# Context normalisation in fewer picks, and its key and value blocks 5.33 picks apart, in a two-layer diffusion backbone

## The reference

```python
for i in range(2):
    hx = hx + gate * mixer_i(modulate(hx, norm1_g[i], shift, scale))
    hx = hx + gate * peer(modulate(hx, norm2_g[i], ...))      # 8 heads x 16 experts of 16384
    if i == 0:
        hc = hc + gate * pool(modulate(hc, ...)); hc = hc + gate * peer(modulate(hc, ...))
# mixer_1 projects both hx and modulate(hc, norm1_g[1], ...) to q, k, v, z, a, b:
#   k, v = silu(conv5(h @ w_in)); decay g = -exp(a_log) * softplus(a + dt_bias); beta = sigmoid(b)
# from the context only k, v, g and beta are needed: its last states start the latents' scan
return rmsnorm(hx, final_g)
```

## Time and profile before

| what | value |
|---|---|
| median of three runs | 2551.62 us |
| the profiled execution's own time | 2557.68 us |
| its span | 2555.7 us |
| TensorE busy (matmul) | 2161.7 us, 85% |
| VectorE busy | 1900.9 us, 74% |
| ScalarE busy | 1103.8 us, 43% |
| GpSimd busy | 921.4 us, 36% |
| mean DMA rate | 361 GB/s |
| granted TensorE clock, mean | 0.976 |

### The profile page before, as it was taken

The page is one execution under the profiler, slowest core; times in us unless marked ns, Lnnn a source line. Parts: engine busy times, 40 slices in busy tenths (PEclk is TensorE's granted clock), DMA queues, the critical chain, the costliest instruction groups (busy, mean ns, idle before and its releaser), DMA issues.

```text
span 2555.7 us, 33277 instructions
## 1 busy us (share of the span) xinstructions
PE 2161.7 (85%) x11048; PEld 1182.1 (46%) x11048; DVE 1900.9 (74%) x5194; ACT 1103.8 (43%) x3063; POOL 921.4 (36%) x902
## 2 busy tenths in 40 slices
PE   7789987787887789888899898998879977777777
PEld 4545542343443344444445457977755522232222
DVE  6667887877877787887887878955577766777674
ACT  5445543433434345554435443633344434344333
POOL 0033333333333435554343434621223333333332
PEclk9899999999999999999999999999989999999999
DMA  9499999999999999999999996800269999999997
GB/s 365 148 403 420 411 421 420 415 408 409 418 408 420 406 405 418 418 418 400 385 381 405 377 400 234 301 19 2 94 266 420 414 422 421 417 417 417 416 411 307
DMA packets 142536, 923.53 MB, mean 361 GB/s; under 512 B 16449, under 2 KB 16609, under 8 KB 43169
## 3 DMA queue, kind: packets, MB, share of 16 engines
q0 software_dynamic: 111696, 810.17, 77.4%
q1 hardware_dynamic: 30672, 111.31, 11.5%
HBM read 920.35 MB, written 1.06 MB: 361 GB/s over the span
## 4 chain that ended last, share of the span: by engine, by line
PE 22%; DMA 20%; DVE 12%; issue 5%; ACT 3%; POOL 2%; POOLq 0%; DVEq 0%
DMA buf<-in_experts,buf 20%; PE pY L2539 12%; DVE buf L1622 5%; PE pY L2299 3%; PE pG L2299 2%; POOL lo L2127 2%; PE pS L2299 1%; PE pS L2271 1%; PE pS L2272 1%; PE pS L2273 1%; ACT buf L813 1%; ACT buf L834 1%; DVE buf L1443 1%; PE pY L2271 1%; PE pY L2272 0%
## 5 line engine op out<-in xcount | busy, mean ns | idle before, releaser
L2539 PE MATMUL pY<-buf 128*128 128x512 f32 x3072 | 1473.5, 614 | 319.3 <-ACT buf L834 316.1
L2108 POOL DMA_INDIRECT buf<-in_experts,buf x768 | 752.0, 979 | 1286.4 <-PE pY L2539 1227.6
L2539 PEld LDWEIGHTS pY<-buf 128*128 128x128 f32 x3072 | 543.2, 191 | 1148.0 <-ACT buf L834 704.1
L1622 DVE SCALAR_TENSOR_TENSOR buf<-pS,buf 128x1024 f32<-128x1024 f32 x384 | 468.5, 1222 | 228.8 <-DMA buf<-in_experts,buf 225.6
L1622 DVE SCALAR_TENSOR_TENSOR buf<-pG,buf 128x1024 f32<-128x1024 f32 x384 | 469.0, 1223 | 223.6 <-DMA buf<-in_experts,buf 218.5
L828 ACT ACTIVATE buf<-buf 128x1 f32<-128x1 f32 x768 | 154.8, 202 | 1034.6 <-DVE buf L1622 1033.3
L813 ACT ACTIVATE buf<-ident,buf 128x128 f32<-128x128 f32 x768 | 296.8, 386 | 0.0
L834 ACT ACTIVATE buf<-buf 128x128 f32<-128x128 f32 x768 | 296.7, 386 | 0.1
L2271 PE MATMUL pY<-h_hi,hi 128*128 128x256 f32 x480 | 151.7, 316 | 8.8 <-DVE h_lo L1278 7.0
L2272 PE MATMUL pY<-h_lo,hi 128*128 128x256 f32 x480 | 137.2, 286 | 0.0
L2273 PE MATMUL pY<-h_hi,lo 128*128 128x256 f32 x480 | 137.1, 286 | 0.0
(11 more groups left out here) (382 smaller groups left out, 2476.4 us busy)
## 6 DMA issues: line engine op xcount, KB each, us to landing
raw<-in_blocks SPq DMA_DIRECT2D x104, 512.0 KB, 7.4
buf<-in_mod_tiles SPq DMA_DIRECT2D x30, 512.0 KB, 5.3
g<-in_mod_tiles SPq DMA_DIRECT2D x26, 512.0 KB, 8.1
buf<-in_experts,buf POOLq DMA_INDIRECT x768, 10.5
raw<-in_mod_wT SPq DMA_DIRECT2D x20, 512.0 KB, 7.3
buf<-in_mod_wT SPq DMA_DIRECT2D x20, 512.0 KB, 8.2
buf<-in_window SPq DMA_DIRECT2D x2, 1024.0 KB, 11.2
buf<-in_keysT POOLq DMA_DIRECT2D x2, 1024.0 KB, 5.1
```

The lines of the kernel that those rows point to most:

```text
L1622: v.scalar_tensor_tensor(x, h_tok[NT * i // NPICK], 1.0, x, ALU.mult, ALU.mult, accum_out=dots[:, i:i + 1]).then_inc(dotted, 1)
L2108: g_.indirect_dma_start(rows_uv[n % ROW_RING].rearrange("p a d -> p (a d)"), None, table, bass.IndirectOffsetOnAxis(expert[:, i:i + 1].bit ...
L2539: mm = t_.matmul(pY[:, 2 * r + hf, :], diags[:, i % DIAG_RING], rows_uv[n % ROW_RING][:, 1, GRP * hf:GRP * hf + GRP], start=(k == 0), stop ...
```

## The change

The context's residual, norm and split take fewer picks of x's call, the first key and value block stands at pick 33 instead of 38, and block `j` stands `16 * j // 3` picks after it instead of `5 * j`: 33, 38, 43, 49, 54, 59, 65, ... 113 for 38, 43, 48, ... 113. The last one stays at 113.

```diff
-NORM_PICK = (96, 22)
+NORM_PICK = (96, 18)
-KV_STEP = 5
+KV_FIRST = 33
 def kv_pick(j):
-    return 38 + KV_STEP * j
+    return KV_FIRST + 16 * j // 3
 # ScalarE
-                    if g == 1 and i == TOPK + 1:
+                    if g == 1 and i == TOPK - 1:
                         norm(4, res[1], lambda: act.wait_ge(fin_ready, 2))
-                    if after and i == (112, 32)[g]:
+                    if after and i == (112, 28)[g]:
                         act.wait_ge(h_tokens, NT * (g + 1))
                         act.wait_ge(normed, 4 + g)
                         h_high(after, 0)
 # VectorE
-                    if g == 1 and i in (12, 15):
-                        q = (i - 12) // 3
+                    if g == 1 and i in (12, 14):
+                        q = (i - 12) // 2
                         ve.wait_ge(y_chan, q + 1)
                         add_branch(res[1], y_half, 0, 5, 1, fin_ready, 4 * q, 4 * q + 4)
-                    if g == 1 and 25 <= i < 31:
-                        norm_ctx(i - 25)
+                    if g == 1 and i in (21, 24, 25, 26):
+                        for part in ((0,), (1,), (2, 3), (4, 5))[(21, 24, 25, 26).index(i)]:
+                            norm_ctx(part)
-                    if after and 0 <= i - (120, 34)[g] < 4:
-                        h_low_part(g + 1, after, i - (120, 34)[g])
+                    if after and 0 <= i - (120, 29)[g] < 4:
+                        h_low_part(g + 1, after, i - (120, 29)[g])
 # TensorE
-                    if i == 35 + r:
+                    if i == 28 + r:
                         pe.wait_ge(normed, 5)
-                    if g == 1 and i in (10, 13):
-                        ctx_transposed((i - 10) // 3)
+                    if g == 1 and i in (10, 12):
+                        ctx_transposed((i - 10) // 2)
```

## The result

The changed kernel is slower by 0.35%: its time is 1.0035 times that before, 95% interval [1.0020, 1.0049]. The medians of six runs each are 2563.61 us (2559.67 to 2570.78) and 2553.02 us (2551.35 to 2562.69); the ratio puts it at +9 us. Forecast were +1.8 us and 2553.4, with a range up to 2560: the time lies outside it, on the side of the second rival.

What follows compares the result with a forecast made beforehand. DMA transfers were taken as the bound. Terms +1.2 + 0.8 + 0.3 - 0.5 = +1.8 us on the median 2551.6 gave 2553.4 us; forecast -1.5 to +4.5 (2550.1 to 2556.1) at 0.62, range 2547 to 2560.

Steps and rivals of the forecast that it cites:

- the second rival: TensorE's wait for `gl_x` before block 1 drains the DMA queue: +5 to +8.5 us, 2556.6 to 2560.1, chance 0.18.
- The bound: From 865 to 1155 us transfers at 423 GB/s are the bound; an ideal schedule could win 6.1 us.
- Norm, +1.2: Picks 15 to 22: mean one pick behind h's transposing, picks 5.7 us late against 4.5; bounds 0 and +3.4.
- First block at 33, second at 38: TensorE waits 3.9 us for `gl_x` behind pick 38, delaying row 45's gather: +0.8 us, bounds 0 and 3.1.
- Then 2.9 us of block: Block 1 on TensorE, right behind the wait at pick 38, was taken to last 2.9 us.
- Row 45's late issue: Gather behind block 1 and pick 39 goes out at 969.3 instead of 966.21, landing at 976.5 to 977.6; costs 0.7 to 1.8.
- Its signs: TensorE stands over 3 us behind pick 38 and row 45 lands more than 9 us after pick 39's end.
- the norm at +3.4: Upper bound for the mean behind h's transposing, picks 17 to 22, if none of that transposing is covered: +3.4 us.
- Blocks 5.33 apart, -0.5: Picks 33 to 113: wider spacing fits TensorE and frees some of 2.8 us; -0.5 us, bounds -2.8 and 0.
- Never on the long step: VectorE's taps fall at picks 4, 5, 9, 10, 14, 15 of a head, avoiding the long step at 7.
- ScalarE at 53 to 57, +0.3: Silu moved from 59 to 55 among six table loads: 15.3 us of work in 13.7 of transfers; bounds 0 and +1.6.
- The signs named beforehand: 865 to 1155 no shorter, deep slices 8 us earlier, TensorE idle behind pick 38, row 45 late, 418 to 423 GB/s from pick 60.

Runs made afterwards that it cites:

- the decay at 34: Changed kernel with VectorE's whole decay step at pick 34 instead of 39, so block 1's bank is free earlier; 1.0015 of before, 2560.91 us.
- the early bank: Changed kernel with only the decay's first product, which reads the a/b bank, moved to step 32 with its own signal; 1.0028 of before, 2564.57 us.
- the decay at 45: Kernel before with the decay at step 45 instead of 39, so block 1 at 43 waits for its bank; 1.0019 of before, 2561.73 us.
- h at 23: The early bank's kernel with h's transposing moved from pick 17 to 23, behind the mean; 1.0017 of before.
- the decay at 44: Kernel before with the decay at step 44 instead of 39, behind block 1 at 43; 1.0000 of before, 2555.62 us.

## Why the prediction was wrong

**The bound: right.** Transfers are; 423 GB/s holds wherever no hole is, and every loss found is a hole of them.

**Norm, +1.2: right.** Picks 18 and 20 and the mean ended as reckoned (910.6, 918.7, 914.1, by the timeline). The stretch lost 2.2 us more, and alone it measures +1.8 us, not clear of zero. That the nearness of two long pieces is the cause can't be shown by time: pulled apart, it stays at 1.0007.

**First block at 33, second at 38, +0.8 with bounds 0 and 3.1: this step failed.** Its wait is there as forecast, 3.67 us for 3.9, released by VectorE. Its price is not: 4.9 us (2.3 to 7.7) put alone into the kernel before, 6.6 us taken out by the decay at 34, 3.3 us (not clear of noise) by the early bank. The holes behind the wait miss 3.6, 5.8 and 4.4 us of transfer in three traces, all above the bound of 3.1. What was mis-sized:

- *The block was priced at full clock.* "Then 2.9 us of block" came from a row in which TensorE had no idle time before it. Behind the wait it took 4.5 us at a granted clock of 0.51 to 0.64 (in the kernel before with the decay at 45, at 0.50, it took 5.5 us from first start to last end, where a block at full clock takes 3.4). The Trainium skill (TensorE: Matmul & The Clock Gate, "What's actually happening") gives an idle TensorE the lower clock. The trace agrees, with 0.51 behind 3.67 us without work. The bounds should have held such a block.
- *Row 45's late issue was taken as 3.1 us.* Pick 39 ended at 973.6, not 968.9, and row 45 went out at 973.96, 7.8 us late. Of this 2.3 us were there at row 44 already; they are about what the norm's hole had cost every row, and are no new loss. (The prediction had named the norm's cost and left VectorE's step at its old time: "the decay, whose last operation ends at 964.16" ended at 967.15, behind a dot of pick 39 that started at 961.33 for 958.68.) The other 5.5 us are the wait's: the 3.1 forecast, 1.6 for the clock, and the rest for VectorE, which ran a little later still and whose cast at L1452 took 0.88 us for 0.33, mostly beside GpSimd's issue of row 44.
- *The price was read off one landing.* The forecast priced the late issue by when row 45 lands. By that measure it was right: with the queue empty the row landed 5.6 us after its issue, sooner than the 7.2 us reckoned with, and so 1.5 us behind where the shift of 2.3 us and one more block put it (978.1), inside the forecast's 0.7 to 1.8. But an empty queue shortens the landing of the first row only. The transfers that should have run in 972 to 976 are missing all the same, 3.6 us of them, and row 46 is 5.9 us later than before where row 45 is 5.0.

The second rival, "the wait for `gl_x` drains the queue", +5 to +8.5 us at 0.18, names what happened: slices of 33 and 4 GB/s. Its signs were badly chosen. TensorE standing over 3 us was already met by the forecast's own 3.9 us. Row 45 landing more than 9 us after pick 39's end did not come: it was 6.0 us (979.55 behind 973.6), since a drained queue makes a landing short and not long. The argument against it, that six row buffers keep bytes in the queue, fails since all six wait for the same TensorE. Its other part, the norm at +3.4, did not come, and its "whole 3.1 us" was too little for the wait.

**Blocks 5.33 apart, -0.5: no gain shows.** With wait and norm accounted for, 1.0015 - 1.0007 = 0.0008 is left of the kernel with the decay at 34, 2 us, within both uncertainties; with the early bank it is 0.0021, 5.4 us. Whether the spacing costs or the move of the blocks to earlier picks can't be told apart: spacing 5 from pick 33 was no better, with a loss of its own behind pick 108. Where the blocks fall within a head seems to matter (a pick later, the rate rises from 403 to 413 GB/s), but the times don't settle it. "Never on the long step" was counted for one engine, while the blocks' parts on ScalarE and GpSimd moved onto others: in the changed kernel VectorE's search met the low parts, and block 10 (pick 86) stood right behind a gate exponential at 85.

**ScalarE at 53 to 57, +0.3: not contradicted.** In the changed kernel itself no dip stands there: from 1005 to 1035 its two traces miss 0.2 and 0.3 us, the kernel before 0.6. With the early bank a hole of 3.1 us stands at 1015 to 1023; with the decay at 34 under 1 us is missing there, with the norm alone nothing. The silu is not the whole cause, as the hole stays when it is moved; what is, stays open.

**The signs named beforehand.** Right: 865 to 1155 no shorter, the deep slices some 10 us earlier, TensorE's idle time and its releaser, row 45 late, no dip near pick 55. Wrong: the slices are deeper than before (57 GB/s where the lowest was 180), and "from pick 60 on 418 to 423 GB/s" fails in the first trace by the hole at 1104. Behind pick 113 the rows catch up by 2.2 us from row 120 to row 152; the kernel with the norm alone, its blocks in their old places, catches up by 3.3, so the blocks are not the reason.

**What stays open.** By the medians the 10.5 us split into 1.8 for the norm, 3 to 7 for the wait and 2 to 5 for the place of the blocks; each part is known no better than to 2 or 3 us. The two ways of removing the wait differ by 3.3 us, within their intervals, and both leave a hole near 972. That a late start from the norm is part of this hole is shown by one trace only (h at 23). The sums of a/b in another bank weren't tried. And 9 us by the ratio stand against 2 us between the two profiles, of which the rows 12 to 120 explain 6.7: single executions differ by several us between the calls too, where this change does nothing.

## What to carry to other kernels

Before a piece of work is moved ahead of a wait that used to be long over, lay out all five engines at the new place: when the signal comes there, what the waiting engine's next piece takes if its clock has fallen, and whether all buffers hang on that engine. Add up everything that is late in the same few microseconds, from the last issue that went out in time, before subtracting the queue's slack. Price a late issue by the transfers that are missing and not by when the late one lands. In these traces the stand-still cost no transfer while it lasted, and showed as a hole in the DMA rate some 5 to 10 us later, so look for the cause ahead of the hole.

And where two executions differ elsewhere by more than the change is worth, compare them over the stretch that it touches, from a gather ahead of it to a gather behind it.

## What the runs showed of the hardware

TensorE's granted clock fell to half behind 3.67 us without work (0.51 from 969 to 971) and behind 4.64 us (0.50 from 980 to 984), in the middle of a busy stretch; the block of 24 matmuls behind it took 1.6 and 2.1 us more. In the changed kernel's second trace, behind 3.67 us again, it started at full clock and fell to 0.50 from 971 to 973.

A gather of 1.055 MB landed 5.6 us after its issue where the queue had run empty (changed kernel, row 45), against 10.3 us in the median from 955 to 1155.

Small VectorE operations can be held for as long as a GpSimd operation lasts. In the changed kernel, VectorE and GpSimd:

```profile
1085.18 3.70 DVE L1375 TENSOR_TENSOR buf<-buf 128x16 f32<-128x16 f32 x5
```

```profile
1085.97 2.79 POOL L2079 TENSOR_TENSOR lo<-raw,hi 128x256 fp32r<-128x256 f32 x4
```

The five took 0.51 us in the kernel before. The Trainium skill (SBUF — State Buffer, "Who interferes with whom") has VectorE and GpSimd share a port pair under an exclusive lock, also for a VectorE operation with two inputs from SBUF; the trace agrees. Here it cost nothing that could be measured. The decay that TensorE waited for was held in the same way: its last three operations took 1.8 us beside the low part (965.32 to 967.15), and 0.7 us with the decay at 44, where no low part ran.
